# Three chunks of the pooling layer's operand go through SyncE's DMA transposes instead of TensorE's

## The reference

```python
h = x
h = h + retention_branch(rms_norm(h, ret_norm), ret_w_in, ret_w_out)      # 8 heads
gate = sigmoid(rms_norm(h, ple_norm[0]) @ ple_w_gate[0])                   # 2048 x 2048
h = h + gate * (p[0] @ ple_w_proj[0])
h = h + pool_branch(rms_norm(h, pool_norm), pool_w_in, pool_w_group, pool_scale, pool_w_out)
...                                                                        # the same gate for layer 1
return rms_norm(h, final_norm)
```

## Time and profile before

| what | value |
|---|---|
| median of 3 runs | 1564.23 us (1564.12 to 1564.25) |
| the profiled execution's own time | 1564.37 us |
| its span in the profile | 1562.6 us |
| TensorE busy | 1550.5 us, 99% |
| VectorE busy | 1020.7 us, 65% |
| ScalarE busy | 842.8 us, 54% |
| DMA transposes | 56 (28 turns), 5.4 us from issue to landing |
| granted TensorE clock | 0.998 |

### The profile page before, as it was taken

The page is one execution under the profiler, slowest core; times in us unless marked ns, Lnnn a source line. Parts: engine busy times, 40 slices in busy tenths (PEclk is TensorE's granted clock), DMA queues, the critical chain, the costliest instruction groups (busy, mean ns, idle before and its releaser), DMA issues.

```text
span 1562.6 us, 18983 instructions
## 1 busy us (share of the span) xinstructions
PE 1550.5 (99%) x6938; PEld 1284.3 (82%) x6938; DVE 1020.7 (65%) x1250; ACT 842.8 (54%) x999; POOL 4.6 (0%) x12
## 2 busy tenths in 40 slices
PE   9999999999999999999999999999999999999997
PEld 7888888888888888888888888888888888888885
DVE  6766666666676676567656585775577557755665
ACT  6465554635455464555645556654664476445553
POOL 0000000000000000000000000000000000000000
PEclk9999999999999999999999999999999999999999
DMA  9575566546556655755455766755765576554451
GB/s 386 210 242 187 176 203 197 204 172 230 189 181 214 197 196 177 229 185 190 160 190 192 198 225 197 238 189 195 224 213 200 188 216 227 213 203 173 178 192 77
DMA packets 102439, 314.73 MB, mean 201 GB/s; under 512 B 63952, under 2 KB 63968, under 8 KB 66816
## 3 DMA queue, kind: packets, MB, share of 16 engines
q1 hardware_dynamic: 101264, 310.02, 57.9%
q0 software_dynamic: 704, 3.27, 0.5%
q10 hardware_dynamic: 432, 0.92, 0.2%
HBM read 297.40 MB, written 2.10 MB: 192 GB/s over the span
## 4 chain that ended last, share of the span: by engine, by line
PE 99%; DVE 1%; ACT 0%; issue 0%; DVEq 0%; ACTq 0%
PE accA L378 12%; PE accA L380 12%; PE accA L379 12%; PE accC L379 11%; PE accC L380 11%; PE accC L378 11%; PE accB L378 8%; PE accB L380 8%; PE accB L379 8%; PE side L394 1%; PE side L613 0%; PE side L433 0%; PE side L432 0%; PE side L431 0%; PE side L422 0%; PE side L423 0%
## 5 line engine op out<-in xcount | busy, mean ns | idle before, releaser
L968 DVE TENSOR_TENSOR w_lo<-w_raw,w_hi 128x1024 fp32r<-128x1024 f32 x550 | 666.6, 1223 | 405.2 <-ACT w_hi L640 403.2
L640 ACT CAST w_hi<-w_raw 128x1024 fp32r<-128x1024 f32 x550 | 574.7, 1053 | 547.6 <-PE accA L380 207.8
L378 PE MATMUL accA<-w_hi,xa_hi 128*128 128x512 f32 x508 | 198.0, 390 | 0.0
L378 PE MATMUL accC<-w_hi,xa_hi 128*128 128x512 f32 x508 | 198.0, 390 | 0.0
L380 PE MATMUL accC<-w_hi,xa_lo 128*128 128x512 f32 x508 | 198.0, 390 | 0.0
L380 PE MATMUL accA<-w_hi,xa_lo 128*128 128x512 f32 x508 | 198.0, 390 | 0.0
L379 PE MATMUL accC<-w_lo,xa_hi 128*128 128x512 f32 x508 | 197.9, 390 | 0.0
L379 PE MATMUL accA<-w_lo,xa_hi 128*128 128x512 f32 x508 | 197.9, 390 | 0.0
L378 PEld LDWEIGHTS accA<-w_hi,xa_hi 128*128 128x128 f32 x508 | 95.4, 188 | 19.7
L380 PEld LDWEIGHTS accC<-w_hi,xa_lo 128*128 128x128 f32 x508 | 95.4, 188 | 19.7
L378 PEld LDWEIGHTS accC<-w_hi,xa_hi 128*128 128x128 f32 x508 | 95.4, 188 | 19.7
(11 more groups left out here) (219 smaller groups left out, 2194.3 us busy)
## 6 DMA issues: line engine op xcount, KB each, us to landing
w_raw<-in_stream_dram SPq DMA_DIRECT2D x275, 1024.0 KB, 4.8
h<-in_x_dram SPq DMA_DIRECT2D x4, 512.0 KB, 14.2
xT_raw<-in_xT_dram SPq DMA_DIRECT2D x3, 512.0 KB, 15.6
dec<-in_decay_dram POOLq DMA_DIRECT2D x1, 1024.0 KB, 9.1
fgain<-in_final_gain_dram POOLq DMA_DIRECT2D x1, 1024.0 KB, 6.7
out_dram<-emb SPq DMA_DIRECT2D x1, 1024.0 KB, 3.8
halvesT<-halves SPq DMA_TRANSPOSE x56, 5.4
w_raw<-in_stream_dram SPq DMA_DIRECT2D x1, 512.0 KB, 6.5
```

The lines of the kernel that those rows point to most:

```text
L378: pe.matmul(acc[pair][t][:, 0:n], xh, wh, start=first and b == 0, stop=False)
L640: act.copy(w_hi[:, r % RING, :], w_raw[:, r // 2, (r % 2) * 1024:(r % 2 + 1) * 1024]).then_inc(hi_ready, 1)
L968: dve.tensor_tensor(w_lo[:, r % RING, :], w_raw[:, r // 2, (r % 2) * 1024:(r % 2 + 1) * 1024], w_hi[:, r % RING, :].bitcast(F32), ALU.subt ...
```

## The change

The transposes of `h` for the pooling layer's operand (stage 2) leave TensorE for three of the four chunks and take the way through the DMA, with buffers of their own (`_r`: in the idle upper halves of `oT_hi` and `oT_lo`, and `words` in the arena). The fourth chunk stays with TensorE. In numbers of units, for chunk c with boundary z:

- ScalarE copies the halves after the split of z+4 (`h_halves`);
- SyncE's two transposes stand ten units behind that place in its list (`AHEAD`), between two pieces;
- ScalarE joins the words and writes `xa_hi` seven units behind the halves (`JOIN[2]`), so after the split of the *next* boundary's unit z+3 (`h_words`), and VectorE writes `xa_lo` at the same place. For chunk 2 that is unit 3 of `group(0, ...)` (`LATE`);
- the two memsets of `sums` move from unit 5 of `close` to unit 4 of the group, behind `row_scale`, since the words lie there now;
- turns are renumbered (`POOL_TURNS`, `CLOSE_TURNS`).

```diff
+Z0 = EMB_U + NC * RO_U
+H_TURNS = (tuple((2, c, Z0 + KD_U * (c + 1) + 4) for c in range(NC - 1)),
+           ())
+BY_PE = [(1, c) for c in range(0, NC)] + [(2, NC - 1)] + [(3, c) for c in range(NC)]
+JOIN = (None, 4, 7)
+AHEAD = 10
+LATE = Z0 + KD_U * (NC - 1) + 4 + JOIN[2] - (Z0 + GATE_U)
...
+            turns = [at_u + AHEAD - at_u % 2 for _stage, _c, at_u in H_TURNS[0]]
+            pieces(CLOSE_A, POOL0, 0, 2 * TURNS, turns[:-1], [in_close[0]] * len(turns[:-1]))
+            pieces(POOL0, POOL1, 0, 2 * POOL_TURNS - 2, (turns[-1] - (POOL0 - CLOSE_A), 20, 28), [in_close[0], in_emb, in_emb])
...
                     for cc in range(NC):
-                        if u == EMB_U + ou * (cc + 1):
+                        if u == EMB_U + ou * (cc + 1) and (2 * layer + 1, cc) in BY_PE:
                             h_transposes(2 * layer + 1, cc)
-                        if cc < NC - 1 and layer == 0 and u == EMB_U + NC * ou + KD_U * (cc + 1) + 1:
-                            h_transposes(2, cc)
...
+            def h_halves(stage, c):
+                act.wait_ge(h_ready, NC * (stage - 1) + c + 1)
+                halves_of(h[:, :, c * COL:(c + 1) * COL], in_close[stage // 3])
+
+            def h_words(stage, c, turn):
+                bufs = in_close[stage // 3]
+                if stage > 1 and c:
+                    act.wait_ge(xT_ready, NC * (stage - 1) + c)
+                words_of(turn, bufs, bufs[2])
+                act.wait_ge(words_ready, turn * 2 + 2)
+                stream_hi(stage, c)
...
+                    if first and u == LATE:
+                        h_words(2, NC - 2, POOL_TURNS - 1)
                     if first and u == 4:
                         stream_hi(2, NC - 1)
...
-                        if u == z + 4 and layer == 0:
-                            stream_hi(2, c)
+                    for i, (stage, c, at_u) in enumerate(H_TURNS[layer]):
+                        if u == at_u + JOIN[stage]:
+                            h_words(stage, c, turn0 + i)
+                        if u == at_u:
+                            h_halves(stage, c)
...
+                    if first and u == LATE:
+                        stream_lo(2, NC - 2)
                     if first and u == 4:
                         stream_lo(2, NC - 1)
                         row_scale(2)
+                        dve.wait_ge(xT_ready, 2 * NC)
+                        for b in sums:
+                            own.mark(dve.memset(b[:, :, 0:PAD], 0.0))
```

More of the change, by code:

```diff
@@ L132, in trunk @@
         xa_lo = sb("xa_lo", [P, KD, SEQ], F32R)
+        oT0 = nc.sbuf_base
         oT_hi = sb("oT_hi", [P, KG, SEQ], F32R)
@@ L137, in trunk, with turn_buffers @@
         emb = sb("emb", [P, TT, D], F32)
-        halves = nc.alloc_sbuf_tensor_at("halves", [P, TT, 2, COL], U16, offset=emb0)
-        halvesT = nc.alloc_sbuf_tensor_at("halvesT", [P, 2 * COL // P, SEQ], U16, offset=emb0 + 4096)
-        words = nc.alloc_sbuf_tensor_at("words", [P, COL // P, SEQ], F32, offset=emb0 + 8192)
+        def turn_buffers(name, a, b, c):
+            return (nc.alloc_sbuf_tensor_at("halves" + name, [P, TT, 2, COL], U16, offset=a),
+                    nc.alloc_sbuf_tensor_at("halvesT" + name, [P, 2 * COL // P, SEQ], U16, offset=b),
+                    nc.alloc_sbuf_tensor_at("words" + name, [P, COL // P, SEQ], F32, offset=c))
+        in_emb = turn_buffers("_e", emb0, emb0 + 4096, emb0 + 8192)
+        words = in_emb[2]
         pT_hi = sb("pT_hi", [P, 2, KP, SEQ], F32R)
@@ L314, in _, with transpose_halves, pieces @@
             next_round(1, 3)
-            def transpose_halves():
+            def transpose_halves(bufs):
                 for t in range(TT):
-                    sp.dma_start_transpose(halvesT[:, :, t * P:(t + 1) * P],
-                                           halves[:, t, :, :].rearrange("p two n -> p (two n)")).then_inc(halvesT_landed, 16)
-            def pieces(u0, u1, loop, n, turns):
+                    sp.dma_start_transpose(bufs[1][:, :, t * P:(t + 1) * P],
+                                           bufs[0][:, t, :, :].rearrange("p two n -> p (two n)")).then_inc(halvesT_landed, 16)
+            def pieces(u0, u1, loop, n, turns, bufs):
                 for q in range(u0 // 2, u1 // 2):
@@ L400, in h_transposes @@
                 pe.wait_ge(h_ready, NC * (stage - 1) + c + 1)
-                if stage + c > 1:
-                    pe.wait_ge(xT_ready, NC * (stage - 1) + c)
+                if stage == 1 and c > 0:
+                    pe.wait_ge(xT_ready, c)
+                if stage == 2:
+                    pe.wait_ge(xT_ready, NC)
+                if stage == 3:
+                    pe.wait_ge(xT_ready, NC * 2 + c)
                 transpose4(lambda t: h[:, t, :], c * COL).then_inc(hT_done, 1)
@@ L658, in stream_hi @@
                 hi = xb_hi if stage % 2 else xa_hi
-                act.wait_ge(hT_done, NC * (stage - 1) + c + 1)
+                if (stage, c) in BY_PE:
+                    act.wait_ge(hT_done, BY_PE.index((stage, c)) + 1)
                 for j in range(4):
                     k = 4 * c + j
-                    cp = act.activation(hi[:, k, :], side[j // 2][:, (j % 2) * SEQ:(j % 2 + 1) * SEQ], ACT.Copy,
-                                        scale=gain[:, stage, k:k + 1])
+                    src = side[j // 2][:, (j % 2) * SEQ:(j % 2 + 1) * SEQ]
+                    if (stage, c) not in BY_PE:
+                        src = in_close[stage // 3][2][:, j, :]
+                    cp = act.activation(hi[:, k, :], src, ACT.Copy, scale=gain[:, stage, k:k + 1])
                     if j % 2:
@@ L692, in pr_hi_part, with halves_of, words_of @@
                 act.copy(pr_hi[:], pr[:]).then_inc(pr_hi_ready, 1)
-            def halves_of(src):
+            def halves_of(src, bufs):
                 for t in range(TT):
-                    act.copy(halves[:, t, :, :], src[:, t, :].bitcast(U16).rearrange("p (n two) -> p two n", two=2)
+                    act.copy(bufs[0][:, t, :, :], src[:, t, :].bitcast(U16).rearrange("p (n two) -> p two n", two=2)
                              ).then_inc(halves_ready, 1)
-            def words_of(n, dst):
+            def words_of(n, bufs, dst):
                 act.wait_ge(halvesT_landed, n * (16 * TT) + 16 * TT)
@@ L704, in words_of @@
                     act.copy(dst[:].bitcast(U16).rearrange("p k (n two) -> p two k n", two=2)[:, i, :, :],
-                             halvesT[:, 4 * i:4 * i + 4, :]).then_inc(words_ready, 1)
+                             bufs[1][:, 4 * i:4 * i + 4, :]).then_inc(words_ready, 1)
+            def h_halves(stage, c):
[8 more added lines that the diff above has]
+                stream_hi(stage, c)
             def qk_halves(hd):
                 act.wait_ge(qk_ready, hd + 1)
-                halves_of(qk)
+                halves_of(qk, in_emb)
             def qk_words(hd):
                 act.wait_ge(yT_ready, hd)
-                words_of(hd * 2 - 1, words)
+                words_of(hd * 2 - 1, in_emb, words)
                 act.wait_ge(words_ready, hd * 4)
@@ L719, in y_halves @@
                 act.wait_ge(y_gated, hd + 1)
-                halves_of(yn)
+                halves_of(yn, in_emb)
             def y_words(hd):
                 act.wait_ge(qkT_ready, hd + 1)
-                words_of(hd * 2, words)
+                words_of(hd * 2, in_emb, words)
                 act.wait_ge(words_ready, hd * 4 + 2)
@@ L771, in u_halves @@
                 act.wait_ge(u_ready, n + 1)
-                halves_of(u)
+                halves_of(u, in_emb)
             def uT_part(n, turn):
@@ L776, in uT_part @@
                     act.wait_ge(d_scaled, n)
-                words_of(turn, uT)
+                words_of(turn, in_emb, uT)
             def m_halves(n, c):
                 act.wait_ge(m_ready, n + 1)
-                halves_of(gm[:, c, :, :])
+                halves_of(gm[:, c, :, :], in_emb)
             def m_words(n, k0, c, turn):
@@ L785, in m_words @@
                     act.wait_ge(mT_ready, n)
-                words_of(turn, words)
+                words_of(turn, in_emb, words)
                 act.wait_ge(words_ready, turn * 2 + 2)
@@ L848, in group @@
                 n2 = g * 2
-                turn = TURNS if first else TURNS - 2 + g * 4
+                turn = POOL_TURNS if first else POOL_TURNS - 2 + g * 4
                 turns = U_FIRST if first else U_LATER
@@ L900, in close @@
                             finished(2 * layer * NC + c, 2 * layer + 1)
-                        if u == EMB_U + ou * (c + 1) + 3:
+                        if u == EMB_U + ou * (c + 1) + 3 and (2 * layer + 1, c) in BY_PE:
                             stream_hi(2 * layer + 1, c)
@@ L1006, in stream_lo @@
                         dve.wait_ge(hT_hi, 2 * (NC * (stage - 1) + c) + j // 2 + 1)
+                    src = side[j // 2][:, (j % 2) * SEQ:(j % 2 + 1) * SEQ]
+                    if (stage, c) not in BY_PE:
```

(12 more changed lines are left out.)

18 lines of the change are left out of this document (11 added, 7 removed).

## The result

The changed kernel takes 1570.57 us in the median of six runs (1569.42 to 1571.05), the kernel before 1564.24 beside it, 6.3 us less: a ratio of 1.0039 with a 95% interval of 1.0029 to 1.0049. The forecast was 1569.7 us, within 1567.0 and 1571.8. The six times are no single group: 1569.42, 1569.44, 1570.09, and three at 1571.04 to 1571.05. The profiled execution belongs to the lower group, with 1569.44 us.

The account below looks back on a forecast made before the run. TensorE, busy 99% of the span, was taken to bound the kernel everywhere. The terms -2.61 + 4.2 + 3.9 gave +5.5 us, so 1569.7 us on the median of 1564.23, with a range of 1567.0 to 1571.8.

Parts of the forecast that it names:

- What TensorE gains: At three boundaries the eight transposes with the restart leave TensorE: 0.87 us each, 2.61 us in all, the most to win.
- The first boundary: Only the halves stand there, 1.89 us in place of 1.44; z+5 is delayed by 0.45 us, covered, so cost nothing.
- The second and third boundary: Words of 4.21 us before the cast of z+4, 2.20 us of margin: 2.1 us lost at each, 4.2 together.
- The last boundary: Behind chunk 3, unit 4 is 1.13 us late and unit 5, behind VectorE's row scale, 2.75 late: together 3.9 us.
- SyncE and the landings: Transposes land by 27.5 us at the latest, the join comes at 30.1: 2.6 us of margin, cost nothing.
- rival 3: TensorE's clock falls in a pause, once more behind the last boundary: 2.7 us lost, 1572.4 us; chance 5%.
- the likeliest case: Joins at the second, third and last boundaries are not covered and TensorE waits: 1569.7 us; chance 76%.
- my own signs of being wrong: No TensorE wait at z+4, ScalarE waiting for the transposes' landing, or matmuls behind pauses further apart than 0.227 us.
- the upper bound of 1571.6: Likeliest case with 4.32 us for the words (0.3 more) and a late xa_lo holding z+4's split (1.6 more, three places).
- Rival 1: At the boundaries the joins are covered and only the transposes' time is seen: 1561.6 us; chance 8%.
- Rival 2: One of the middle two boundaries is covered after all, by an unseen rhythm: 1567.6 us; chance 6%.
- rival 4: A landing or piece comes too late; each us beyond 2.6 of margin costs one at three joins: 1572 or more; 5%.

Follow-up runs that it names:

- The last experiment: Against the kernel before: all three chunks through the DMA, joined behind z+6 and the pooling layer's unit 1, row scale behind unit 7; 1561.46 us against 1564.19, ratio 0.9982.

## Why the prediction was right, point by point

The measured 1570.57 us lies inside the forecast's range, and each term of its sum came out within 0.3 us. The clock, which the sum put at nothing, did not, and part of the agreement is luck; both are said below.

- **What TensorE gains.** 0.87 us a chunk, 2.61 in all. The last experiment, where nothing else is late, gives 2.7. Right.
- **The first boundary costs nothing.** No wait there in the changed kernel, and from the first boundary to the second are 21.76 us (769.47 to 791.23) where 21.8 was forecast. Right.
- **The second and third boundary, 2.1 us each.** On the changed kernel's timeline the pause before z+4, less one matmul, with the slower starts behind it: 2.11 - 0.23 + 0.10 + 0.10 = 2.1 and 2.10 - 0.23 + 0.11 + 0.05 = 2.0. The 4.21 us of the words were 801.64 - 797.43 = 4.21. Right.
- **The last boundary, 3.9 us.** Before unit 4 1.32 - 0.23 + 0.07 = 1.2 (forecast 1.13), before unit 5 2.62 - 0.23 + 0.10 = 2.5 (forecast 2.75). The term was 0.2 too large, about half of it by the memsets: from the last row-scale instruction to unit 5's split it was 0.28 us (855.55 to 855.83), where the timeline of before had 0.20 (850.18 to 850.38), so the two cost 0.08 and not 0.2. The experiment with the row scale later confirms the mechanism: -2.4 us, as worked out.
- **The sum.** 2.1 + 2.0 + 1.2 + 2.5 - 2.6 = +5.2; the lower group lies at 1569.4, which is +5.2. Forecast +5.5.
- **SyncE and the landings cost nothing.** No copy of words waited for a landing, though the landings in this stretch took 6.1 to 7.8 us, 7.0 in the median, and not the 5.4 of all turns. The experiments with the joins elsewhere keep the transfers and lose the cost. Right.
- **The clock (rival 3)** is the step that was mis-sized. I gave it 5% and 2.7 us, taken from the start of the kernel, where the profile's granted clock is 1.00, so that no row shows this price to be the clock's. The fall happens in about half of the executions (five of eleven over both sets of runs, with one more, 1570.09, in between that no trace explains) and costs 1.6 us. It comes on top of the likeliest case, and is why the median of the first six runs is 1570.57 and not 1569.4. One of my own signs of being wrong came true with it: behind the pause of 2.63 us matmuls start 0.43 us apart and not 0.227.
- **Luck.** The range held these runs for another reason than it gave. Of the 1.9 us between the forecast and the upper bound of 1571.6, 1.6 were for an `xa_lo` that ends late and holds the split of z+4. That did not happen: at the boundary behind chunk 1 it ended at 802.65 (800.97 + 1.68), and the split started at 802.71, 1.07 behind the cast's start where 1.06 was counted. The fall of the clock, which the range left out, is of the same size and took that place. Five further runs of the same kernel had their median at 1569.51.
- **Rival 1**, the joins are covered, did not occur in the change. It holds at another place: where the join stands in the middle of a chunk, the same 4.2 us are covered in full.
- **Rival 2**, one boundary is covered, and **rival 4**, a late landing, did not occur either.

## What to carry to other kernels

Between engines that run one list through a ring, a piece of work has no price of its own: it has the price of the place. Lay the timelines over each other and ask at the place how early the next split is (2.2 us here) and how long the inserted work holds it (4.2 us); the same work three units later cost nothing, and one unit later it still made a pause of 2.21 us. Follow the delay to the end of the *slowest list behind it*, not only to the next split: twice (in the change and with all three chunks joined outside the clump) the last wait was for VectorE, behind a row scale that nobody needed for another six units. And where TensorE is the bound, a pause may cost more than its length, by the clock behind it: here pauses of 2.21 and 2.62 us did in about half of the executions.

## What the hardware showed unexpectedly

- A pause of TensorE of 2.2 to 2.6 us inside dense work took its clock from 2.4 to 1.2 GHz in some executions of the same program and not in others: 5 of 11 with one of 2.21 us, 4 of 8 with one of 2.62 us (and one of 1.30 a unit before), 0 of 11 where the longest were 2.11 and 2.10. The counts go by the groups of times; two traces show the fall itself. Each fall cost 1.5 to 1.7 us, held eight or so matmuls (858.16 to 861.52 in the profile that shows it best), and began 0.6 us (806.81 to 807.44) and 1.0 us (857.13 to 858.16) *after* work was taken up again. What decides in which executions it comes stays open.
- A restart of TensorE behind a wait for VectorE costs about 0.15 to 0.2 us beyond the wait: it starts 0.05 us after VectorE's end, and the matmul behind the first comes 0.33 us later instead of 0.227.
